# Routing steps, one-hot batches, coefficients and scratch transfers re-dealt in a two-layer decoder kernel

## The reference

```python
def peer_ffn(h, w_q, keys_1, keys_2, expert_u, expert_v):
    q = (h @ w_q).reshape(b, s, PEER_HEADS, 2, PEER_HALF)
    s1 = jnp.einsum('bshd,hkd->bshk', q[..., 0, :], keys_1)
    s2 = jnp.einsum('bshd,hkd->bshk', q[..., 1, :], keys_2)
    v1, i1 = lax.top_k(s1, PEER_TOPK)
    v2, i2 = lax.top_k(s2, PEER_TOPK)
    ...
    top_sc, pos = lax.top_k(cand_sc, PEER_TOPK)
    ids = jnp.take_along_axis(cand_id, pos, axis=-1)
    g = jax.nn.softmax(top_sc, axis=-1)
    ...
    act = jax.nn.gelu(jnp.einsum('ced,cd->ce', u, hx), approximate=False)
    return jnp.einsum('ce,ced->cd', gx * act, vv)
```

## Time and profile before

| | us |
|---|---|
| median of three runs | 4781.25 (4781.08 to 4782.48) |
| the profiled execution | 4780.19 |
| its span (first to last instruction) | 4778.5 |
| TensorE busy | 4114.4 (86%) |
| VectorE busy | 2312.9 (48%) |
| ScalarE busy | 1776.4 (37%) |
| GpSimd busy | 957.7 (20%) |
| all 16 transfer engines, queue of SP | 50.0% of the span |
| mean granted TensorE clock | 0.926 |

### The profile page before, as it was taken

How to read it: one execution, slowest core, us unless ns; L and a number is a source line. 1 busy time by engine, 2 the same in 40 slices (tenths; PEclk the granted TensorE clock), 3 DMA queues, 4 the chain that set the end, 5 groups by cost and what they waited for, 6 DMA issues and landing times.

```text
span 4778.5 us, 50402 instructions
## 1 busy us (share of the span) xinstructions
PE 4114.4 (86%) x20142; PEld 3419.8 (72%) x20142; DVE 2312.9 (48%) x4301; ACT 1776.4 (37%) x2124; POOL 957.7 (20%) x422
## 2 busy tenths in 40 slices
PE   7988887788779999999898887887788998888887
PEld 6867766667667877777676776766667776666666
DVE  4444775555554444444446477555555433333333
ACT  3344333333334444434433423333333333333333
POOL 1232441111111222222110143111111111111111
PEclk9999998888889999999988999988888999999999
DMA  4533443455456766666432434445555765555553
GB/s 181 185 128 115 150 147 137 158 166 160 153 179 203 256 223 220 224 225 224 172 122 82 150 129 149 141 150 163 167 161 168 215 223 191 187 194 183 187 190 136
DMA packets 279163, 823.34 MB, mean 172 GB/s; under 512 B 146064, under 2 KB 178832, under 8 KB 195216
## 3 DMA queue, kind: packets, MB, share of 16 engines
q1 hardware_dynamic: 278496, 816.96, 50.0%
q10 hardware_dynamic: 432, 3.15, 0.2%
HBM read 750.84 MB, written 69.21 MB: 172 GB/s over the span
## 4 chain that ended last, share of the span: by engine, by line
PE 78%; DVE 9%; issue 9%; ACT 3%; POOL 0%; DMA 0%; DVEq 0%; SPq 0%; ACTq 0%; POOLq 0%
PE bank L1168 24%; PE bank L1167 12%; PE bank L1296 10%; PE bank L1300 10%; PE bank L1298 10%; PE bank L1188 2%; PE bank L1190 2%; DVE lo L684 2%; PE bank L1189 2%; ACT hi L473 2%; DVE wa L886 1%; PE bank L1267 1%; PE bank L1268 1%; DVE match L824 1%; PE bank L1170 1%
## 5 line engine op out<-in xcount | busy, mean ns | idle before, releaser
L473 ACT ACTIVATE hi<-raw 128x1024 fp32r<-128x1024 f32 x1294 | 1366.2, 1059 | 2440.4 <-PE bank L1168 1225.1
L684 DVE TENSOR_TENSOR lo<-raw,hi 128x1024 fp32r<-128x1024 f32 x919 | 1139.1, 1240 | 2077.4 <-ACT hi L473 2077.0
L1168 PE MATMUL bank<-act_t,hi 128*128 128x512 f32 x5120 | 1868.2, 411 | 23.2 <-DVE stage L689 17.7
L437 POOL TENSOR_TENSOR lo<-raw,hi 128x1024 fp32r<-128x1024 f32 x375 | 916.3, 2444 | 3746.5 <-ACT hi L473 3746.5
L1167 PE MATMUL bank<-act_t,lo 128*128 128x256 f32 x4800 | 1403.9, 292 | 0.0
L1168 PEld LDWEIGHTS bank<-act_t,hi 128*128 128x128 f32 x5120 | 990.1, 198 | 243.0 <-DVE stage L689 20.6
L1167 PEld LDWEIGHTS bank<-act_t,lo 128*128 128x128 f32 x4800 | 961.0, 200 | 13.5
L1296 PE MATMUL bank<-hi,wa 128*128 128x512 f32 x2048 | 672.3, 410 | 141.0 <-DVE wa L886 134.9
L1298 PE MATMUL bank<-lo,wa 128*128 128x512 f32 x2048 | 662.1, 405 | 0.0
L1300 PE MATMUL bank<-hi,wa 128*128 128x512 f32 x2048 | 661.5, 405 | 0.0
L1296 PEld LDWEIGHTS bank<-hi,wa 128*128 128x128 f32 x2048 | 393.5, 195 | 260.9 <-DVE wa L886 161.8
(11 more groups left out here) (208 smaller groups left out, 2348.4 us busy)
## 6 DMA issues: line engine op xcount, KB each, us to landing
raw<-in_stream SPq DMA_DIRECT2D x647, 1024.0 KB, 4.8
act_rows<-stage SPq DMA_DIRECT2D x64, 512.0 KB, 6.7
w_rows<-w_stage SPq DMA_DIRECT2D x64, 512.0 KB, 7.5
acts<-act_rows SPq DMA_DIRECT2D x64, 512.0 KB, 5.7
w_part<-w_rows SPq DMA_DIRECT2D x64, 512.0 KB, 6.7
x_res<-in_x SPq DMA_DIRECT2D x2, 1024.0 KB, 6.0
keys_sb<-in_keys ACTq DMA_DIRECT2D x2, 1024.0 KB, 4.8
out<-xn SPq DMA_DIRECT2D x2, 1024.0 KB, 4.0
```

The costliest lines, as they stand in the source:

```text
L437: pool.tensor_tensor(lo[:, s, :], raw[:, n0 % RAW_SLOTS, j * HALF:(j + 1) * HALF], hi[:, s, :].bitcast(F32), ALU.subtract).then_inc(lo_rea ...
L473: act.activation(hi[:, s, :], raw[:, slot, j * HALF:(j + 1) * HALF], ACT.Copy).then_inc(hi_ready[s], 1)
L684: dve.tensor_tensor(lo[:, s, :], raw[:, n0 % RAW_SLOTS, j * HALF:(j + 1) * HALF], hi[:, s, :].bitcast(F32), ALU.subtract).then_inc(lo_read ...
L1168: ins = mm(ps[:], w_hi, act_t[:, kt, :, :].rearrange("p w t -> p (w t)"), start=first, stop=last)
```

## The change

- **Routing dealt out.** DVE's routing work becomes `route_step`, one step per unit: the two searches of a head in two units and its pair search (`route_pairs`) in the third, starting at unit 2 of `wq`; so 24 steps cover units 2 to 25 (16 `wq` units and tiles 0 to 9). Decoding takes tiles 10 to 23, the turn of the selections tile 25. `pq_t` holds all 16 units. GpSimd's larger share of the subtractions lasts until tile 27 (it was 9).
- **One-hots in batches.** A batch takes four DVE instructions on 128 x 1024 float16 elements. The tokens are the inner index, so TensorE reads its operands at a step of eight elements. Batches are made at two of every three tiles from tile 26 on (the last at tile 72; it was 103), and TensorE takes a batch three tiles after it was made (it was one), ACT four.
- **Coefficients one unit earlier.** `weigh`, `coefficients_hi` and `coefficients_lo` move to the first, second and third unit of a group.
- **Scratch transfers on ACT.** The functions `store_acts`, `store_weights` and `load_group` move from SP's program into ACT's. One piece of `w_stage` is stored per tile, in eight tiles of each twelve. SP only loads units.

```diff
-BATCH_TILE = 10
-BATCH_STEP = 3
+BATCH_TILE = 26
+BUILD_LAG = 3
...
-TURN_TILE = 7
-EXP_TILE = 3
+ROUTE_AT = 2
+DECODE_AT = ROUTE_AT + 3 * 8
+TURN_AT = 41
+EXP_TILE = 12
...
 def batch_at(tile):
-    b, off = divmod(tile - BATCH_TILE, BATCH_STEP)
-    return b if off == 0 and 0 <= b < BATCHES else None
+    three, r = divmod(tile - BATCH_TILE, 3)
+    b = 2 * three + r
+    return b if r < 2 and 0 <= b < BATCHES else None
...
+        iota_rep = place("iota_rep", 67, [P, NKEYS, BATCH], F16)
+        hot1 = place("hot1", 69, [P, NKEYS, BATCH], F16)
+        hot2 = place("hot2", 71, [P, 2, NKEYS, BATCH], F16)
+        hot1g = place("hot1g", 75, [P, 2, 2, NKEYS, BATCH], F16)
...
-            busy = any(U0[f"wq{k}"] + LEAD <= n0 < U0[f"peer{k}"] + TURN_TILE + 3 + LEAD for k in range(2))
+            busy = any(U0[f"wq{k}"] + LEAD <= n0 < U0[f"peer{k}"] + BATCH_TILE + LEAD for k in range(2))
...
@@ ScalarE, peer @@
                 for j in range(TILES):
-                    if batch_at(j - 2) is not None:
-                        stage_weights(batch_at(j - 2))
+                    b = batch_at(j - BUILD_LAG - 1)
+                    if b is not None:
+                        stage_weights(b)
                     split_hi(base + j + LEAD)
-                    if j == TILES - GROUP + 2:
+                    if j % GROUP == 1 and j > GROUP:
+                        store_acts(layer, j // GROUP - 1)
+                    for f in range(FLUSHES):
+                        piece = j - last_batch_tile(f) - BUILD_LAG - 2
+                        if 0 <= piece < PIECES:
+                            store_weights(layer, f, piece)
+                    if j == TILES - GROUP - 2:
+                        load_group(layer, 0)
+                        load_group(layer, 1)
+                    if j == TILES - GROUP + 1:
                         coefficients_hi(0)
                     gelu(j)
...
-                    if i == 2 and g + 1 < GROUPS:
+                    if i == 1 and g + 1 < GROUPS:
                         coefficients_hi(g + 1)
                     split_hi(out0 + t + LEAD)
+                    if t == 0:
+                        store_acts(layer, GROUPS - 1)
+                        load_group(layer, 2)
+                    if i == 3 and g + 3 < GROUPS:
+                        load_group(layer, g + 3)
@@ VectorE @@
+            def route_step(layer, i):
+                n, r = divmod(i - ROUTE_AT, 3)
+                if 0 <= n < PEER_HEADS:
+                    if r < 2:
+                        route_unit(layer, 2 * n + r)
+                    else:
+                        route_pairs(n)
+                n = i - DECODE_AT
+                if n == 0:
+                    start_decoding(layer)
+                elif 1 <= n <= 12:
+                    w, r = divmod(n - 1, 6)
+                    if r < 4:
+                        decode(w, 4 * r, 4 * r + 4)
+                    else:
+                        sum_places(w, r - 4)
...
                 def one_hots(b):
-                    for t in range(BATCH):
-                        tok = BATCH * b + t
-                        dve.tensor_scalar(hot2[:, b % 2, t, :], iota[:], sel_t[:, 1, tok:tok + 1], None, ALU.is_equal)
-                        for w in range(2):
-                            ins = dve.tensor_scalar(hot1g[:, b % 2, t, w, :], iota[:], sel_t[:, 0, tok:tok + 1],
-                                                    sel_t[:, 2 + w, tok:tok + 1], ALU.is_equal, ALU.mult)
+                    dve.tensor_tensor(hot2[:, b % 2, :, :], iota_rep[:],
+                                      i2_t[:, tok].unsqueeze(1).to_broadcast([P, NKEYS, BATCH]), ALU.is_equal)
...
+                    dve.tensor_tensor(hot1[:], iota_rep[:], i1_t[:, tok].unsqueeze(1).to_broadcast([P, NKEYS, BATCH]),
+                                      ALU.is_equal).then_inc(hot1_ready, 1)
+                    dve.wait_ge(hot1_ready, done + 1)
+                    for w in range(2):
+                        ins = dve.tensor_tensor(hot1g[:, b % 2, w, :, :], hot1[:],
+                                                g_parts[:, w, tok].unsqueeze(1).to_broadcast([P, NKEYS, BATCH]), ALU.mult)
...
-                        if i == 1:
+                        if i == 0:
                             weigh(g + 1)
-                        elif i == 3:
+                        elif i == 2:
                             coefficients_lo(g + 1)
@@ TensorE, build_w and its caller @@
-                        mm(o, hot2[:, b % 2, t, :], hot1g[:, b % 2, t, 0, :], start=True, stop=False)
+                        mm(o, hot2[:, b % 2, :, t], hot1g[:, b % 2, 0, :, t], start=True, stop=False)
...
-                    b = batch_at(j - 1)
+                    i, b = 2 * PEER_HEADS + j, batch_at(j - BUILD_LAG)
```

More of the change, by code:

```diff
@@ L217, in build_program @@
         keys_sb = place("keys_sb", 0, [P, 2 * PEER_HEADS, NKEYS])
-        pq_t = place("pq_t", 8, [P, 2, S])
+        pq_t = place("pq_t", 48, [P, 2 * PEER_HEADS, S])
         top_v = place("top_v", 10, [P, NC_TOK, PEER_HEADS, 2, TOPK])
@@ L396, in _ @@
-            for n in range(U0["peer0"]):
+            for n in range(N_UNITS):
                 load(n)
-            peer(0)
-            for n in range(U0["c"], U0["peer1"]):
-                load(n)
-            peer(1)
             for c in range(NC_TOK):
@@ L537, in output_hi, with store_acts, store_weights, load_group @@
                 act.activation(act_t[:, h, 0, :], ps_b[(b0 + h) % 2][0][:, 0:S], ACT.Copy).then_inc(ot_hi, 1)
+            def store_acts(layer, g):
+                act.wait_ge(gelu_done, layer * TILES + GROUP * (g + 1))
+                at = GROUP * (g % 2)
+                act.dma_start(a_dram[layer][g], stage[:, at:at + GROUP, :].rearrange("p h t -> p (h t)")).then_inc(
+                    a_stored[g % 2], 16)
+            def store_weights(layer, f, piece):
+                act.wait_ge(w_free, layer * BATCHES + FLUSH * (f + 1))
+                at, i = FLUSH_TOK * f, PIECE * piece
+                act.dma_start(w_dram[layer][i:i + PIECE, :, at:at + FLUSH_TOK].rearrange("i p t -> p i t"),
+                             w_stage[f % 2][:, i:i + PIECE, :]).then_inc(w_stored[f % 2], 16)
+            def load_group(layer, g):
+                if g == 0:
+                    for f in range(2):
+                        act.wait_ge(w_stored[f], 16 * PIECES * (layer + 1) * (FLUSHES // 2))
+                act.wait_ge(a_stored[g % 2], 16 * (layer * (GROUPS // 2) + g // 2 + 1))
+                if g >= 2:
+                    act.wait_ge(wa_lo, layer * GROUPS + g - 1)
+                act.dma_start(acts[g % 2][:].rearrange("p h t -> p (h t)"), a_dram[layer][g]).then_inc(aw_in[g % 2], 16)
+                act.dma_start(w_part[g % 2][:], w_dram[layer][GROUP * g:GROUP * (g + 1)].rearrange(
+                    "h p t -> p h t")).then_inc(aw_in[g % 2], 16)
             def peer(layer):
@@ L1251, in keys_product, with key_unit, routing @@
                 for c in range(NC_TOK):
-                    ins = mm(ps_c[idx % 2][:, c * P:(c + 1) * P], pq_t[:, u % 2, c * P:(c + 1) * P], keys_sb[:, u, :],
+                    ins = mm(ps_c[idx % 2][:, c * P:(c + 1) * P], pq_t[:, u, c * P:(c + 1) * P], keys_sb[:, u, :],
                              start=True, stop=True)
                 ins.then_inc(c_full, 1)
+            def key_unit(i):
+                n, r = divmod(i - ROUTE_AT, 3)
+                return 2 * n + r if r < 2 and 0 <= n < PEER_HEADS else None
+            def routing(layer):
+                for i in range(2 * PEER_HEADS):
+                    u = key_unit(i)
+                    unit_a(U0[f"wq{layer}"] + i, A0[f"wq{layer}"] + i,
+                           middle=(lambda u=u: keys_product(layer, u)) if u is not None else None)
             def peer(layer):
@@ L1313, in peer @@
                     out_unit(t)
-            def routing(layer):
-                for u in range(2 * PEER_HEADS):
-                    unit_a(U0[f"wq{layer}"] + u, A0[f"wq{layer}"] + u,
-                           middle=(lambda u=u: keys_product(layer, u - 1)) if u else None)
             pe.wait_ge(consts, N_CONSTS)
```

128 lines of the change are left out of this document (37 added, 91 removed).

## The result

| | median of the runs | against before |
|---|---|---|
| before | 4781.16 us (4780.12 to 4782.48, 4 runs) | |
| the change | 4307.65 us (4307.29 to 4309.28, 4 runs) | 0.901 (95%: 0.8995 to 0.9026) |
| forecast | 4105 us (4045 to 4230) | |

The change is faster by 473.5 us, where the forecast said 676. It is 203 us short, and outside the range.

The account below looks back on a forecast made before the run. The prediction took TensorE as the bound, with the gain in its gaps and the slow clock behind them: 4780.2 us less 472.3 (stretches 1 and 2) and 203.1 (stretch 3) gives 4104.8, stated as 4105 us, range 4045 to 4230.

Parts of the forecast that it names:

- The price p of a batch: TensorE, stretches 1 and 2: sixteen products at 0.107 us cost 1.71 us per batch, 54.8 us for 32 batches.
- The keys products: TensorE, stretches 1 and 2: 16 keys products at 0.60 us add 9.6 us per layer.
- Rival B: Batch products on TensorE: the step of eight costs more, 0.214 us per product, giving 4214 us; chance 15 in 100.
- Gaps ahead of the batches: TensorE ahead of each batch's first product: 313.8 us idle in 62 waits for VectorE's one-hots, expected to vanish.
- Clock 1.00 through stretches 1 and 2: TensorE's granted clock, 0.89 before where batches run, was to be 1.00 from `wq` to the end of stretch 3.
- VectorE's cost: Batch tiles: one-hots at 1.22 us each, with sums and splits 17.4 of 20.4 us per three tiles, so hidden.
- rival C: Batch tiles: VectorE becomes the bound, one-hots held 1.2 us beyond the margin, 77 us, giving 4182 us; chance 8 in 100.
- ScalarE's issues at nothing: Stretches 2 and 3: ACT's 256 extra transfer issues cost nothing, as ACT needs 13.3 of 20.4 us per three tiles.
- Rival D: ACT is held by transfer issues of 2.86 us, delaying TensorE 156 us, giving 4261 us; chance 8 in 100.
- Stretch 3: Earlier coefficients end TensorE's wait per group of four units: groups 22.41 us apart, gain 203.1 us over both layers.
- Rival E: The wait in stretch 3 stays because ACT-issued loads land too late, giving 4308 us; chance 3 in 100.
- Rival F: Slower than before: the step of eight makes batch products eat all gain, from 0.77 us per product; 4873 us; 2 in 100.

Follow-up runs that it names:

- dense_both: The changed kernel with both operands of the batch products stored densely (tokens outer, keys innermost): 4100.45 us, ratio 0.8578.
- small_hots: The changed kernel with the earlier kernel's 24 small one-hot instructions per batch, in its dense layout: 4109.87 us.
- dense_pool: dense_both with GpSimd's larger share of the subtractions kept until the last batch: 4147.95 us.
- after_sp: The changed kernel with the scratch's stores and loads issued by SP again, at the same places in the order: 4308.19 us.
- coef_only: The kernel before with only the three coefficient steps moved one unit earlier: 4572.08 us.
- split_build: The changed kernel with each batch's sixteen TensorE products given in two parts of eight, one in each half of the unit: 4222.06 us.

## Why the prediction was wrong

- **The price p of a batch: the step that failed.** The prediction took 0.107 us per product, from a row at the lower clock, and called it a factor of two for the step at full clock. The runs show 0.235 us, four times the dense 0.056, and above the upper bound of 0.214. That is 16 x (0.235 - 0.107) = 2.05 us per batch. Missing from the sum altogether was what slow products do to the clock, 1.34 us more per batch. Together that is the measured 5.10 - 1.71 = 3.39 us, and 64 of these are 217 us.
- **The keys products: mis-sized, by luck the other way.** The 0.60 us of the earlier trace rows is the duration of four overlapping products; each group adds 0.34 us. That is 4.2 us per layer too much and hides 8 of the 217 us; 208.3 are left as the miss in stretches 1 and 2.
- **Rival B** had the right mechanism and too small a price. Every element in a line of its own was the worst that the layout allows, and no row justified stopping at twice the slow one. The passage of the Trainium skill that it names as its reason also counts 8 bf16 as a free stride, which the prediction left out; the 0.235 us against 0.056 speak against that half of it. The range had no room for the clock, although the prediction itself, in its first part, tells how the clock falls behind gaps.
- **Gaps ahead of the batches: right.** None is left, and nothing else took their place. That VectorE needs 8.2 us per batch was a wrong reading: 24 overlapping instructions take 5.0 us, close to TensorE's gap of 5.11 us.
- **Clock 1.00 through stretches 1 and 2: wrong,** 0.88 to 0.90 where batches run, by the same cause.
- **Routing: right.** Its steps hide beside the sums: 88.1 us in each layer.
- **VectorE's cost: right side, wrong size.** 1.22 us per one-hot was taken, 0.68 measured without GpSimd beside it (one of four takes 1.76 us in the mean, held). The estimate of 0.69 us that the prediction worked out from the Trainium skill, "VectorE: DVE Perf Modes", its perf-mode tier table, was the better one. The price of that pace is TensorE's step of eight, and the prediction treated the two as unrelated. The hold by GpSimd was foreseen (rival C) and is seen in `dense_both`, `small_hots` and `dense_pool`.
- **ScalarE's issues at nothing: right.** `after_sp` differs by 0.5 us, and no `w_rows` issue on ACT takes the 2.86 us. Rival D is refuted.
- **Stretch 3: right.** 22.36 us per group; `coef_only` gains 209 us where 203.1 were forecast.
- **Rival E** gives the measured number and is wrong. The wait for `wa` is gone; its 203 us and the 208 us missed in stretches 1 and 2 are alike by chance. A total that fits proves no cause.
- **Rival F:** the price per product is 0.235 us, 0.13 more than the row, far from its 0.77. (The 675 us of this rival are the gain with 1.71 us per batch paid, not without a price.)

## What to carry to other kernels

Before a layout is turned to please one engine, ask which engine bounds the kernel and how that one will read it. Here TensorE pays for the step in 16 products per batch, and what VectorE gained was time for which TensorE had hardly waited. A layout between the two extremes, a step of two 16-bit elements, kept TensorE at full rate at little cost for VectorE. When no row has a price, ask for the worst case that the layout allows, and add what the slowness does to the clock. Where a change has several parts, run each by itself: the largest gain here (some 387 us) lies in the tiles with batches, by their new order, and one part cost 198 us under cover of the rest.

## What the runs showed of the hardware that was not expected

- A streamed float16 operand costs 0.057, 0.119, 0.235 and 0.237 us per 128 columns at steps of 2, 4, 8 and 16 elements. For the loaded operand a step of eight costs next to nothing here: its load goes from 98 to 148 ns in the trace, and the products go from 0.056 to 0.062 us apart.
- TensorE without any gap can lose its clock: behind 3.7 us of products 0.235 us apart the granted clock fell to 0.50, 1.2 GHz; behind 1.9 us of the same products (`split_build`) it stayed at 1.00.
- VectorE's two-input float16 instruction on 1024 elements takes 0.68 us with a repeated operand whose innermost run is eight or four values, 1.08 us for the comparison at two (but 0.69 for the multiplication that reads `hot1`), and 1.22 us where one value is repeated innermost. Why comparison and multiplication differ at two was not looked into.
